# Another order for the prologue of a hybrid decoder step on one core: parameter columns, panel splits, norm roots and first products

## What is computed

```python
def chunk_gmlp(xn, w_in, ln_g, ln_b, w_s, b_s, w_out):     # xn = rms_norm(h, g_norm[0])
    u, v, gate = jnp.split(xn @ w_in, 3, axis=-1)          # w_in: 1024 x 6144, v: 544 x 2048
    v = layer_norm(v, ln_g, ln_b)
    ...
    s = jnp.einsum('gts,bnsgc->bntgc', ws, vc) + b_s[:, :c].T[None, None, :, :, None]
    y = (u * s * jax.nn.silu(gate)) @ w_out
def rms_norm(x, g):
    y = x32 * lax.rsqrt(jnp.mean(x32 * x32, axis=-1, keepdims=True) + EPS)
    return (y * g.astype(jnp.float32)).astype(x.dtype)
```

## Time and profile before

| | us |
|---|---|
| median of 3 runs | 1160.44 |
| lowest, highest | 1160.05, 1162.42 |
| the profiled execution, its own time | 1161.06 |
| its span, first to last instruction | 1159.3 |
| PE busy, matmuls | 1089.7 (94%) |
| DVE, ACT, POOL busy | 630.8, 438.0, 400.4 |
| mean granted TensorE clock | 0.956 |

### The profile page before, as it was taken

How to read it: one execution, slowest core, us unless ns; L and a number is a source line. 1 busy time by engine, 2 the same in 40 slices (tenths; PEclk the granted TensorE clock), 3 DMA queues, 4 the chain that set the end, 5 groups by cost and what they waited for, 6 DMA issues and landing times.

```text
span 1159.3 us, 20936 instructions
## 1 busy us (share of the span) xinstructions
PE 1089.7 (94%) x7896; PEld 988.3 (85%) x7896; DVE 630.8 (54%) x798; ACT 438.0 (38%) x654; POOL 400.4 (35%) x260
## 2 busy tenths in 40 slices
PE   4899979999999989999799999999689999999996
PEld 4799969999999989999798888898366776679996
DVE  6645545553345546655567656656446565436634
ACT  4111135442133332423344555654543544312421
POOL 6152056632255514346331122100025453604331
PEclk8999989999999989999899999999779999989998
DMA  8322202233322242322232222131427566432201
GB/s 224 109 70 76 72 25 84 72 90 101 91 56 74 70 128 73 91 73 59 70 92 74 84 81 83 50 103 29 143 73 252 183 217 217 129 89 76 73 1 77
DMA packets 152867, 111.17 MB, mean 96 GB/s; under 512 B 4482, under 2 KB 138770, under 8 KB 152722
## 3 DMA queue, kind: packets, MB, share of 16 engines
q1 hardware_dynamic: 152818, 110.49, 31.7%
HBM read 103.53 MB, written 6.95 MB: 95 GB/s over the span
## 4 chain that ended last, share of the span: by engine, by line
PE 89%; DVE 6%; ACT 2%; issue 1%; POOL 1%; DMA 0%; DVEq 0%; ACTq 0%; POOLq 0%
PE acc L1187 61%; PE ob L1469 4%; PE acc L1453 3%; PE zb L1506 2%; PE zb L1370 2%; PE ob L1506 2%; PE ob L1397 2%; PE ob L1386 2%; PE zb L1515 1%; PE acc L1351 1%; PE zb L1318 1%; DVE vt L1715 1%; PE zb L1489 1%; PE acc L1586 1%; PE zb L1477 1%
## 5 line engine op out<-in xcount | busy, mean ns | idle before, releaser
L1187 PE MATMUL acc<-act_hi,w_hi 128*128 128x272 f32 x1904 | 406.5, 295 | 18.2 <-DVE w_lo L1603 7.6
L1187 PE MATMUL acc<-act_hi,w_lo 128*128 128x272 f32 x1904 | 396.8, 290 | 0.0
L1187 PE MATMUL acc<-act_lo,w_hi 128*128 128x272 f32 x1904 | 396.2, 290 | 0.0
L1187 PEld LDWEIGHTS acc<-act_hi,w_hi 128*128 128x128 f32 x1904 | 301.9, 191 | 24.1 <-issue 9.9
L1187 PEld LDWEIGHTS acc<-act_lo,w_hi 128*128 128x128 f32 x1904 | 302.9, 191 | 0.0
L1187 PEld LDWEIGHTS acc<-act_hi,w_lo 128*128 128x128 f32 x1904 | 300.8, 191 | 0.0
L689 POOL TENSOR_TENSOR raw<-raw,cols 128x1024 f32<-128x1024 f32 x80 | 164.6, 2067 | 229.9 <-DMA raw<-in_w_in_b_dram 95.7
L1603 DVE TENSOR_TENSOR w_lo<-raw,w_hi 128x1024 fp32r<-128x1024 f32 x120 | 179.8, 1499 | 36.1 <-ACT w_hi L870 35.1
L870 ACT ACTIVATE w_hi<-raw 128x1024 fp32r<-128x1024 f32 x120 | 126.9, 1060 | 187.2 <-PE acc L1187 129.9
L839 POOL TENSOR_TENSOR vp_lo<-vpage,vp_hi 128x2048 fp32r<-128x2048 f32 x16 | 72.8, 4553 | 62.0 <-ACT vp_hi L1135 62.0
L1864 DVE TENSOR_TENSOR_SCAN left<-rest,zeros 128x512 f32<-128x512 f32 (+3 forms) x64 | 54.2, 847 | 47.0 <-ACT rest L1025 47.0
(11 more groups left out here) (264 smaller groups left out, 1393.9 us busy)
## 6 DMA issues: line engine op xcount, KB each, us to landing
raw<-in_w_in_a_dram SPq DMA_DIRECT2D x48, 512.0 KB, 3.9
kpage<-in_cache_k_dram SPq DMA_DIRECT2D x32, 512.0 KB, 4.8
vpage<-in_cache_v_dram SPq DMA_DIRECT2D x64, 256.0 KB, 3.2
raw<-in_w_out_a_dram SPq DMA_DIRECT2D x16, 512.0 KB, 3.9
raw<-in_w_ple_gate_dram SPq DMA_DIRECT2D x16, 512.0 KB, 3.9
raw<-in_w_kv_dram SPq DMA_DIRECT2D x16, 512.0 KB, 4.1
raw<-in_w_in_b_dram SPq DMA_DIRECT2D x16, 512.0 KB, 4.2
raw<-in_w_out_b_dram SPq DMA_DIRECT2D x8, 512.0 KB, 4.2
```

What stands on the lines that cost most here:

```text
L1187: mm = pe.matmul(t[:, c, 0:TH], wt[:, s, kt, :], xt[:, kt, c * TH:(c + 1) * TH], start=start and kt == kts[0] and wt is w_hi and xt is xh, ...
```

## The change

1. DVE copies `cols` ahead of `lo_tokens` of the fourth full block (and of the small one, as it did), in place of behind the fourth block's.
2. DVE splits panels 0, 1 and 2 before the roots, where it split only panel 0; the roots then stand behind all three. PE spreads the roots in the middle of panel 1's products, after 24 of its 48 matmuls, in place of between panels 0 and 1.
3. In the first group, DVE reads product k first and splits panel 3 + k after it, in place of the other way round. Later groups keep their order.

No arithmetic, transfer or buffer is added or removed.

```diff
             def value_tiles(first=False):
                 for k in range(SLOTS + 1):
-                    if k < SLOTS:
+                    if first and k == 1:
+                        pe.wait_ge(lo_made, panel.now(1))
+                        t = take_acc()
+                        products(t, panel.slot(SLOTS), act_hi[0], act_lo[0], range(KT // 2), True, False)
+                        spread_roots()
+                        products(t, panel.slot(SLOTS), act_hi[0], act_lo[0], range(KT // 2, KT), False, True)\
+                            .then_inc(panel_done, 1)
+                        panel.step()
+                    elif k < SLOTS:
                         gemm(0)
-                    if first and k == 0:
-                        spread_roots()
                     if k > 0:
...
-                if c > 0:
+                if 0 < c < QB:
                     lo_tokens(c - 1)
 
             t = turn()
             dve.tensor_copy(cols[:, :], t[:, 0, 0:N_COL]).then_inc(acc_read, 1)
+            lo_tokens(QB - 1)
             lo_tokens(QB)
-            split_next()
+            for _ in range(AHEAD):
+                split_next()
             dve.wait_ge(const_set, 9)
             dve.wait_ge(x_squared, TT)
             column_roots(rms_s[:, 3, :])
             dve.engine_nop().then_inc(roots_made, 1)
-            for _ in range(AHEAD - 1):
-                split_next()
             dve.wait_ge(rinv_made, 1)
 
-            def value_tiles(i):
+            def value_tiles(i, first=False):
                 for k in range(SLOTS + 1):
                     if k < SLOTS:
-                        split_next()
+                        if not first:
+                            split_next()
                         t = product()
                         dve.tensor_tensor(halves(vt[:, k % 2, :]), both(t), halves(rinv[:, :]), ALU.mult)\
                             .then_inc(acc_read, 1)
+                        if first:
+                            split_next()
...
-            value_tiles(0)
+            value_tiles(0, True)
```

## The result

| | before | after |
|---|---|---|
| median of 11 runs, us | 1161.06 | 1164.0 |
| lowest, highest | 1157.01, 1162.5 | 1161.81, 1165.46 |
| span of the profiled execution | 1159.3 | 1162.2 |
| mean granted clock | 0.956 | 0.957 |

The ratio is 1.0027, with a 95% interval of 1.0016 to 1.0038: the change costs 3.1 us (1.9 to 4.4). A second measurement of the same kernel beside its variants gave 1.0023 (1.0013 to 1.0034).

A forecast was written before the change was run, and what follows sets the result against it. PE, holding 89% of the chain that ended last, was taken as the bound. 0 + 2.1 - 0.2 + 1.1 = +3.0 us gave a median of 1163.4; +1.6 for the clock gave 1165.0, range 1161.0 to 1166.2.

The forecast's parts named there:

- the sum without the clock: All three parts' effects on PE's time together, 0 + 2.1 - 0.2 + 1.1 = +3.0 us, giving a median of 1163.4.
- the clock holds: Rival: PE's granted clock does not fall through the new wait ahead of the roots; 1163.4 us, chance 0.26.
- One line of work for DVE and POOL: DVE instructions reading and writing SBUF and POOL scales never run side by side; 1.9 us per scale, 1.1 per split.
- the rule of the Trainium skill: A VectorE instruction with two SBUF inputs and a GpSimd instruction reading SBUF exclude each other; first to issue keeps the ports.
- Part 1 at 0: Copying `cols` earlier leaves PE's start of panel 0 as it was: 0 us, between -0.15 and +0.1.
- Part 2, a wait of 2.1 us: In mid panel 1 PE waits for the roots, through at 35.0 as two scales cut in: +2.1 us.
- Part 3, +1.13: At the first group's end split 6 loses its cover, landing behind product 3's read where PE waits: +1.13 us.
- The sign that I named: At the first group's end, PE's wait for `ws_t` would be about 4.1 us in place of 3.02.
- Part 3, -0.2: Ahead of panel 2, product 1 is read without split 4 in front: 1.13 us between panels becomes 0.9, -0.2 us.
- The clock, +1.6: PE's wait ahead of the roots drops the granted clock to half, costing +1.6 us; held likelier, 60 to 40.

## Why the prediction was right or wrong

The time lies in the range, and slower was right. The predicted 1165.0 is 1.0 us above the 1164.0 measured, but some of this closeness is luck. The forecast of the difference was 3.0 + 1.6 = 4.6 us, on a median of 1160.44 from three runs; measured were 3.1 us on 1161.06 from eleven. So the difference was 1.5 us too large, and the base 0.6 too low. That the sum without the clock, 3.0 us, is within 0.1 of the 3.1 doesn't mean that the clock held: by its number the rival *the clock holds*, at 1163.4, is nearer than the forecast, and the trace excludes it. In the two stages the forecast of 4.6 us is what the traces show, 4.63.

- **One line of work for DVE and POOL: right.** Removing the scales brings all root instructions to 0.17 us, removing scale 1 brings split 0 from 1.81 to 1.23 us. In this the rule of the Trainium skill (SBUF — State Buffer, Who interferes with whom) is borne out for the splits, which have two inputs in SBUF. The held-up root instructions of 1.86 and 1.77 us are TENSOR_SCALARs with one input in SBUF, so the two inputs that the prediction names in the rule are not what all of them have in common.
- **Part 1 at 0: right within its bounds,** -0.15 us, the bound itself.
- **Part 2, a wait of 2.1 us: right,** 2.20 in one profile and 1.54 in the other; the roots were through at 34.77, forecast 35.0, with the scale of panel 4 in front of them and panels 5 and 6 cutting in. Panel 6's met the tenth of the thirteen instructions, where about seven were forecast to be left; the place makes no difference to the sum. That the size varies with PE's arrival after the first half-clock stretch I had not counted.
- **Part 3, +1.13: mis-sized by 0.15.** It is +0.98 in stage B. With split 6 in front, the copies of the last tile no longer wait for PE: in DVE's timeline the second tile's copies start 0.74 us after the first one's long copy before (52.68 to 53.42, the rows below), and 0.60 us after it now (57.42 to 58.02). I said that no idle time of that length lies in DVE's stretch, and overlooked a shorter one. The sign that I named, a wait for `ws_t` of about 4.1 us, is not there as such: PE waits 1.24 us ahead of the turned mixing matrices (0.23 before) and then 2.76 us for `ws_t` (3.02 before).
- **Part 3, -0.2: mis-sized.** It is -0.07, the difference of the two waits in the earlier trace rows (0.43 and 0.36), which I had in hand. I took the 1.13 us between panels against 0.9, with the end of a matmul counted in one and not in the other.
- **The clock, +1.6: the mechanism right, its worth at the end too high.** The fall came in all four profiles with the wait (waits of 1.54 to 2.20 us), in none without it, and costs 1.5 us in the stage. Filling the wait brings the stage back, and the time by 0 to 0.8 us. The 4.6 us of the stages lie above both measured intervals (up to 4.4 and up to 3.9 us), so part of them is gone by the end.

DVE's copies of the last two tiles before, for part 3:

```profile
52.68 0.67 DVE L1722 COPY v_nat<-acc 128x512 f32<-128x512 f32 x1
53.42 0.28 DVE L1721 COPY v_nat<-acc 32x128 f32<-32x128 f32 x1
```

Where the clock's 1.5 us go shows in how far the changed kernel lags at later waits of PE. Before:

```profile
152.66 2.08 PE L1293 MATMUL acc<-ws_t,ones 128*128 128x512 f32 x2 [5.83 <-DVE ws_ts L1751]
425.93 0.82 PE L1187 MATMUL acc<-act_hi,w_hi 128*128 128x272 f32 x2 [3.62 <-DVE p_t L1771]
556.83 1.12 PE L1221 MATMUL acc<-ident,kt_t 128*128 128x128 f32 x4 [5.41 <-DVE kt_t L1911]
1006.82 1.10 PE L1489 MATMUL zb<-sp_n,negones 32*128 32x64 f32 x8 [1.83 <-DVE sp_b L1971]
```

After:

```profile
156.46 2.08 PE L1299 MATMUL acc<-ws_t,ones 128*128 128x512 f32 x2 [5.83 <-DVE ws_ts L1760]
430.81 0.52 PE L1187 MATMUL acc<-act_hi,w_hi 128*128 128x272 f32 x2 [3.62 <-DVE p_t L1780]
560.58 1.12 PE L1221 MATMUL acc<-ident,kt_t 128*128 128x128 f32 x4 [5.41 <-DVE kt_t L1920]
1010.05 1.10 PE L1495 MATMUL zb<-sp_n,negones 32*128 32x64 f32 x8 [1.83 <-DVE sp_b L1980]
```

The waits are equal, but the lag is 4.59 us at panel 4, then 3.80, 4.88, 3.75 and 3.23, and 2.9 at the end of the span. It changes after waits in which the clock fell in both kernels: behind panel 4's start the clock is at half until 63.2 before (5.2 us of work) and until 66.0 after (3.4 us). How long a half-clock stretch lasts thus differs between executions, and one more fall shifts all that come later. The mean granted clock of all runs points the same way. One more fall of 3.4 us would lower it by 0.0015 (an estimate, 3.4 / 2 of 1160 us); it is 0.9567 over the 19 runs of the changed kernel and 0.9570 over 82 runs of the kernel before (a single one at 0.912 left out). And at equal mean clock the changed kernel is slower by 2.4 to 3.6 us: 1165.2 against 1162.1 at 0.954, 1163.8 against 1160.9 at 0.956, 1163.9 against 1160.2 at 0.957, 1161.9 against 1159.5 at 0.96. That is about what the waits give without the clock. So much of the fall seems to be given back by shorter half-clock stretches elsewhere. That is argued from these means and not shown by a run of its own, and what decides how long a stretch lasts stays open.

## What to carry to other kernels

Before moving an instruction, ask what its completion releases and where that lands: here three early splits freed three buffers, and the scales that followed cut straight into the tiny instructions that PE was about to need. Where two engines exclude each other, reordering one of them may be worth next to nothing (0.15 us of 1.13 here) unless the other is reordered too, and a chain of small dependent instructions belongs where the other engine has nothing to do. And look first at what precedes the instruction that the bounding engine waits for: moving two copies ahead of the statistics was worth more than all three parts could have brought, and saved a fall of the clock as well. Last, a saving read in one stage is not yet one at the end: a start 0.9 us earlier and a fall of the clock worth 1.5 us both left no trace that the times can tell.

## What the runs showed of the hardware that was not expected

With a wait of only 1.54 us between dense matmuls the granted clock fell to half, and it fell when PE was already busy again: 2.0 and 2.3 us after it had resumed in the two profiles with this wait, 0.4 us after in the changed kernel with its 2.20 us, where the clock was at half from 35.3 to 38.7 us. Filled with matmuls, the same wait left it at 1.00; the one wait of 1.29 us ahead of panel 2 left it at 1.00 too. Back-to-back scales let a chain of dependent root instructions take one step per scale (1.84, 1.82, 1.81, 1.82 us for work of 0.17), so a chain of thirteen can grow from 2.4 to 9 us.
